# RWKV-7 recurrence on one Trainium2 core: state steps moved into the windows, forward group n beside backward group 0, 4, 3, 2, 1

## The reference

```python
def _rwkv7_step(state, inp):
    r, w, k, v, kk, a = inp
    sa = jnp.einsum("dbhvk,dbhk->dbhv", state, kk)
    state = (state * w[..., None, :] - sa[..., None] * (kk * a)[..., None, :]
             + v[..., None] * k[..., None, :])
    return state, jnp.einsum("dbhvk,dbhk->dbhv", state, r)
...
    _, y = lax.scan(_rwkv7_step, s0, (shared(r), to_scan(decay), to_scan(k_dir),
                                      shared(v), shared(kk), to_scan(iclr)))
    y = y[0] + _seg_flip(y[1], n_ctx, 1)
```

## Time and profile before

| | us |
|---|---|
| median of three executions | 6579.88 |
| the profiled execution, own time | 6581.77 |
| its span (first to last instruction) | 6579.9 |
| its mean granted TensorE clock | 0.935 of full |
| busy in the span: TensorE | 5670.6 (86%) |
| busy: VectorE / ScalarE / GpSimd | 2987.5 / 2063.0 / 1877.6 |

### The profile page before, as it was taken

One profiled execution on the slowest core, in us unless ns is written; L12 is line 12 of the kernel. 1 busy time (PEld: TensorE's weight loads), 2 busy tenths in 40 slices (PEclk: granted clock), 3 DMA queues, 4 the chain that ended last, 5 costly groups with the idle time before them and its releaser, 6 DMA issues. The chain is left out here.

```text
span 6579.9 us, 214205 instructions
## 1 busy us (share of the span) xinstructions
PE 5670.6 (86%) x92720; PEld 3807.5 (58%) x92720; DVE 2987.5 (45%) x6387; ACT 2063.0 (31%) x3451; POOL 1877.6 (29%) x2006
## 2 busy tenths in 40 slices
PE   5999788888887899977888895698999888888887
PEld 4555577777774455444554454544454677777773
DVE  7100366666663233145534367522300466666661
ACT  3000255454541312133422132311100354544440
POOL 4452144444441336000002631000000344444440
PEclk8999899999998999988899997899999899999998
DMA  3222100001112222122212237522112001110002
GB/s 130 100 90 84 45 31 31 31 31 43 36 37 76 106 100 79 44 84 68 60 48 91 95 96 96 127 72 85 65 65 74 35 31 39 37 39 31 31 31 93
DMA packets 192660, 425.81 MB, mean 65 GB/s; under 512 B 24384, under 2 KB 108224, under 8 KB 192192
## 3 DMA queue, kind: packets, MB, share of 16 engines
q1 hardware_dynamic: 157440, 322.85, 16.5%
q10 hardware_dynamic: 34752, 96.51, 3.7%
HBM read 313.41 MB, written 105.87 MB: 64 GB/s over the span
## 5 line engine op out<-in xcount | busy, mean ns | idle before, releaser
L382 PE MATMUL ps<-arena 128*128 128x512 f32 x4544 | 1686.0, 533 | 60.4 <-ACT arena L336 18.4
L382 PEld LDWEIGHTS ps<-arena 128*128 128x128 f32 x4544 | 862.9, 190 | 878.7 <-issue 810.5
L1890 PE MATMUL ps<-arena 64*64 64x64 f32 x35840 | 737.1, 226 | 172.1 <-issue 75.9
L158 POOL TENSOR_TENSOR arena<-arena 128x512 f32<-128x512 f32 (+1 forms) x360 | 338.9, 957 | 1700.3 <-DMA arena<-w_mod 1690.1
L1890 PEld LDWEIGHTS ps<-arena 64*64 64x64 f32 x35840 | 644.3, 138 | 244.7 <-issue 229.9
L2297 ACT COPY arena<-ps 128x512 f32<-128x512 f32 (+1 forms) x880 | 535.8, 626 | 411.7 <-PE ps L1890 403.1
L2442 POOL TENSOR_TENSOR arena<-arena 128x256 f32<-128x256 f32 (+1 forms) x320 | 316.6, 997 | 812.5 <-DVE arena L2683 533.7
L540 PE MATMUL ps<-arena 128*128 128x512 f32 (+1 forms) x1152 | 422.9, 527 | 18.2 <-ACT arena L336 18.2
L2367 POOL MEMSET arena<- 128x1280 f32 (+4 forms) x22 | 15.1, 739 | 1331.2 <-POOLq L88 1331.2
L161 POOL TENSOR_TENSOR arena<-arena 128x256 f32<-128x256 f32 (+2 forms) x504 | 376.5, 759 | 51.2 <-issue 0.2
L1698 ACT COPY arena<-ps 128x1280 f32<-128x1280 f32 (+1 forms) x64 | 75.0, 1172 | 963.5 <-PE ps L382 749.0
(11 more groups left out here) (269 smaller groups left out, 9762.3 us busy)
## 6 DMA issues: line engine op xcount, KB each, us to landing
arena<-proj SPq DMA_DIRECT2D x158, 640.0 KB, 5.1
proj<-arena ACTq DMA_DIRECT2D x80, 640.0 KB, 3.8
arena<-w_mod SPq DMA_DIRECT2D x96, 512.0 KB, 7.4
arena<-rw_w SPq DMA_DIRECT2D x68, 512.0 KB, 3.4
xres<-arena ACTq DMA_DIRECT2D x24, 640.0 KB, 6.1
arena<-na_w_in SPq DMA_DIRECT2D x24, 512.0 KB, 3.6
arena<-x SPq DMA_DIRECT2D x16, 640.0 KB, 6.7
arena<-xres SPq DMA_DIRECT2D x16, 640.0 KB, 6.0
```

The source lines that it names most:

```text
L158: self.nc.gpsimd.tensor_tensor(out, strip[:, c:c + n, :], self.k.cond[:, c:c + n, s:s + 1].to_broadcast([P, n, P]), ALU.mult)
L382: last = nc.tensor.matmul(k.ps[:, 3 * u + n, 0:b - a], w[:, c * P:(c + 1) * P], src[:, c, a:b], start=(c == 0), stop=(c == KT - 1))
L1890: last = PE.matmul(part_of(out, dst, hh, g, d), part(l, src, hh, g, d), rhs, start=True, stop=True)
```

## The change

It does the following in rwkv_recur; the diff is cut to its core.

- Window n of a tile now holds chunk group n in the forward direction and group BACK[n] = 0, 4, 3, 2, 1 in the backward one. So the order of the windows is the order of both recurrences.
- The state loop is gone. The four state steps of a window's chunks are issued in the next turn, between the products of that window; a last set of them stands behind the last tile. Each step has the same eight matmuls as before. The states restart at zero at each tile (restart()).
- Because the two directions of a window lie on different tokens, V is kept for both (four transposes of v in place of two) and local_outputs() goes per direction: 64 matmuls in place of 56 (16 chunks and directions). GpSimd no longer sums M3; it adds the second touch of y instead (second_outputs()).
- turned_scores() multiplies BH against KK and R in one set of sixteen 128-column matmuls; the set of 64 columns for the receptances (m4) is gone.
- Both halves of the negated gh, and the negated zt, are done by ScalarE; before, one half and zt were VectorE's.
- x4 also waits for nt_ev, f1 for y4_ev, kv for y_ev.
- Between two tiles there remain the projections, the key norm, the first operands and the normalisation of the tile before, in an order of their own. weighted() and finished() go to windows 0 and 1, the product of bonus_terms() to windows 2 and 3, gate_values() to window 0.
- The first tile's preparation is in the same loop body; LOOP_FILL is 70 in layer 0 and 69 in layer 3.

```diff
-LOOP_FILL = (0, 24)
+BACK = (0, 4, 3, 2, 1)
+LOOP_FILL = (70, 69)
...
+            def step(n):
+                for d in range(2):
+                    at, col = map_of(d, n) * C, chunk_of(d, n) * C
+                    for hp in HP:
+                        PE.matmul(state_reads(d)[hp, col:col + C], Sst[hp, n % 2, d, :], QT[hp, at:at + C], start=True, stop=True)
+                    for hp in HP:
+                        last = PE.matmul(state_sums(d)[hp, :], TT[hp, at:at + C], Sst[hp, n % 2, d, :], start=True, stop=True)
+                    last.then_inc(s_mm[d], 1)
...
             def turned_scores():
-                scores(low[1], BH_, KK_).then_inc(xt_mm, 1)
+                for d in range(2):
+                    for g in range(2):
+                        for hh in range(2):
+                            for c in range(2):
+                                at, col = (2 * g + c) * C, (g * 2 + d) * C
+                                last = PE.matmul(halves(pair[1][HP[c], hh, :])[:, :, col:col + C], ops[HP[hh], BH_, d, at:at + C],
+                                                 ops[HP[hh], KK_:R_ + 1, d, at:at + C], start=True, stop=True)
+                last.then_inc(xt_mm, 1)
...
                 pe.wait_ge(gh_ev, it + 1)
-                pe.wait_ge(gh1_ev, it + 1)
                 transitions()
                 pe.wait_ge(x2_ev, it + 1)
                 pe.wait_ge(x2t_ev, it + 1)
+                pe.wait_ge(nt_ev, it + 1)
                 product(low[0], B1, B0, 1).then_inc(x4_mm, 1)
-                pe.wait_ge(nt_ev, it + 1)
-                pe.wait_ge(m3_summed, it + 1)
                 local_outputs()
                 pe.wait_ge(y2_ready, it + 1)
                 pe.wait_ge(f0_ready, it + 1)
+                pe.wait_ge(y4_ev, it + 1)
-                product(low[3], Ya, F, 1).then_inc(f1_mm, 1)
+                product(low[0], Ya, F, 1).then_inc(f1_mm, 1)
...
                 product(low[0], Yb, F, 2).then_inc(f2_mm, 1)
-                scores(low[1], BH_, R_).then_inc(m4_mm, 1)
...
+                pe.wait_ge(yw_ev, it + 1)
+                pe.wait_ge(q_ev, it + 1)
+                step(0)
                 pe.wait_ge(f2_ev, it + 1)
                 product(low[0], F, None, 3).then_inc(di_mm, 1)
+                states_seen(it, 1)
+                step(1)
...
                 product(low[0], A0, NT, 4).then_inc(z_mm, 1)
                 product(low[1], NT, A0, 4).then_inc(zt_mm, 1)
+                states_seen(it, 2)
+                step(2)
...
                 product(low[1], B0, B1, 5).then_inc(z2t_mm, 1)
                 product(low[0], B1, B0, 5).then_inc(z2_mm, 1)
+                states_seen(it, 3)
+                step(3)
                 product(low[2], Ya, F, 5).then_inc(f3_mm, 1)
+                pe.wait_ge(y_ev, it + 2)
+                pe.wait_ge(v_kept, it + 1)
...
                 product(low[0], A0, A1, 6).then_inc(z4_mm, 1)
-                product(low[3], Yb, F, 6).then_inc(f4_mm, 1)
+                product(low[1], Yb, F, 6).then_inc(f4_mm, 1)
                 first_scores()
...
                 product(low[2], Ya, F, 7).then_inc(f5_mm, 1)
                 turned_scores()
...
+                    carried(late, it)
                     eyed(Yb, low[0]).then_inc(y4_ev, 1)
+                    queries(it)
+                    masked(M4, high[1], k.m_i).then_inc(m4_ev, 1)
                     masked(M1, low[2], k.m_s)
                     masked(M3, high[2], k.m_i).then_inc(m3_ev, 1)
+                    step(late, it, 0)
+                    step(late, it, 1)
+                    if n == 0:
+                        weighted(e)
+                    if n == 1:
+                        finished(e)
                     if n + 2 < NW2:
                         sums_scan(e, n + 2)
+                    step(late, it, 2)
                     if more:
                         operands_beta(e, n + 1)
-                    V.tensor_scalar(wide(B1), low[1], -1.0, None, ALU.mult).then_inc(zt_ev, 1)
+                    if n:
+                        step(late, it, 3)
+                    else:
+                        restart(it)
+                    state_outputs(late)
```

More of the change, by code:

```diff
@@ new lines, in queries, with step @@
+            def queries(it):
+                if it > 1:
+                    dve.wait_ge(r_kept, it - 1)
+                dve.wait_ge(yw_ev, it)
+                hold(k, dve)
+                V.tensor_tensor(QT.rearrange("p (c q) -> p c q", c=2), pair[3][:, :, 4 * C:8 * C],
+                                Rk.rearrange("p (c q) -> p c q", c=2), ALU.add).then_inc(q_ev, 1)
+            def step(unit, it, n):
+                for d in range(2):
+                    q = map_of(d, n)
+                    dve.wait_ge(s_mm[d], (it - 1) * 4 + (n + 1))
+                    V.scalar_tensor_tensor(Sst[:, (n + 1) % 2, d, :], state_sums(d), pc[:, unit, q:q + 1],
+                                           KHs[:, q * C:(q + 1) * C], ALU.mult, ALU.add).then_inc(s_ev[d], 1)
@@ L2627, in _, with restart, state_outputs @@
+            def restart(it):
+                for d in range(2):
+                    dve.wait_ge(s_mm[d], it * 4)
+                    V.memset(Sst[:, 0, d, :], 0.0).then_inc(s_ev[d], 1)
+            def state_outputs(unit):
+                for d in range(2):
+                    at = outputs_to(d, unit)
+                    V.tensor_tensor(at, at, state_reads(d), ALU.add)
+                dve.drain().then_inc(y_ev, 1)
+            kk_scaled(0)
             dve.wait_ge(zeroed, 1)
             for e in range(KT):
-                def eyed(out, in_):
-                    return V.tensor_tensor(out.rearrange("p (h q c) -> p h q c", h=2, c=C), in_.rearrange("p h (q c) -> p h q c", c=C),
-                                           k.eye2.unsqueeze(1).unsqueeze(1).to_broadcast([P, 2, 4, C]), ALU.add)
@@ new lines, in _ @@
+                sums_scan(e, 0)
+                sums_rest(e, 0)
+                for c in range(3):
+                    centred(e, MEAN_BANK, c)
+                for c in range(3):
+                    kk_unit(e, c)
+                bonus(e, BONUS_BANK, 0)
+                operands_beta(e, 0)
+                operands_kk(e, 0)
+                variance(e, VAR_BANK)
+                operands_r(e, 0)
+                bonus(e, BONUS_BANK, 1)
+                bonus(e, BONUS_BANK, 2)
+                post_inverse(e)
@@ L2739, in _ @@
+                for c in range(3):
+                    scaled(e, SCALE_BANK, c)
+                mask_scores(e, 0)
+                mask_turned(e, 0)
+                mask_rest()
+                operands_keys(e, 0)
+                sums_scan(e, 1)
+                sums_rest(e, 1)
                 for n in range(NW2):
                     window(n)
-                step(1)
-                kk_inverse(e + 1)
-                step(2)
-                carried(NW2 - 1)
-                step(3)
-                queries(NW2 - 1)
@@ L2793, in _ @@
-                mask_rest()
-                operands_keys(e + 1, 0)
-                sums(e + 1, 1)
+            it = KT * NW2 + 1
+            carried(NW2 - 1, it)
+            for c in range(3):
+                centred(KT, MEAN_BEFORE, c)
+            queries(it)
+            for n in range(4):
+                step(NW2 - 1, it, n)
+            state_outputs(NW2 - 1)
+            for c in range(3):
+                bonus(KT, BONUS_BEFORE, c)
+            variance(KT, VAR_BEFORE)
+            post_inverse(KT)
```

877 lines of the change are left out of this document (378 added, 499 removed).

## The result

The changed kernel took 7324.03 us (median of four executions, 7307.09 to 7337.58), the kernel before beside it 6577.11 us; the ratio is 1.1135 [1.111, 1.1159]. The forecast was 6532 us with a range of 6420 to 6650; the result lies far outside, and no rival reached it. The profiled execution took 7337.58 us, its span is 7335.4 us.

The account below looks back on a forecast made before the run. TensorE was taken to bound the windows. Per layer +3 (start), -147.7 (between tiles), +8.8 (window 0), +144 (windows 1 to 4), -32 (end): -23.9; twice, -48 from 6581.8 gives 6534, median 6532 us, range 6420 to 6650.

Parts of the forecast that it names:

- the window's sum: Windows 1 to 4: 19.7 us of TensorE work plus 4.4 of waits, 24.1, taken as 23.8 against 19.3 before.
- the slowest: Rival: state steps wait for each other and cost 1.3 us each, as alone; +224 us, 6756 us, chance 0.04.
- gh of window 4 to gh of the next window 0: Stretch across a tile boundary: 26.5 us between tiles and 30 for window 0, forecast 56.5 us.
- The walk of a window: New order followed from x2 through windows 1 to 4, wait by wait; new waits of 4.4 us in all.
- the sentence on GpSimd's 3 us instructions: Windows 0, 2 and 3 would lose something to GpSimd sharing SBUF interfaces with VectorE; no size given.
- The rival of VectorE's row: VectorE's late work behind step 3 leaves TensorE idle; 25.0 us a window, +96 us, 6628 us, chance 0.17.
- Full windows: Rival: windows about as full of TensorE work as before, 22.3 us each; -120 us, 6412 us, chance 0.26.
- Between the tiles: From gh's end to x2, a chain without the 19 steps: 26.5 us against 47.6 before, bounds 23 and 34.
- The low-clock rival: Half clock through the between-tiles chain into window 0; projections 7 us more a tile, +98 us, 6630 us, chance 0.09.
- Window 0: First window of a tile: 30 us against 28.9 before, including some 3.5 us of stalls on "issue".
- The start of a layer: First tile's preparation becomes the longer chain: +3 us a layer; filling matmuls taken as covered by loads and memsets.
- The end of a layer: From a layer's last window to the output projection: 60 us against 91.8 before, -32 us a layer.

Follow-up runs that it names:

- e3: Changed kernel with LOOP_FILL (77, 39) for (70, 69), placing both layers' window bodies within seven pieces of 256 instructions; 6676.93 us, ratio 1.0144.
- e6: e5 with TensorE's w group issued ahead of first_scores() in every window; 6605.48 us, ratio 1.0035.
- e9: e6 with gate_values() moved from window 0 to window 1 and LOOP_FILL (13, 39) for (77, 39); 6554.24 us, ratio 0.9955.
- e8: e7 with the four projections put ahead of the sums of norms on TensorE between tiles; 6641.89 us, ratio 1.0085.
- e5: e3 with GpSimd's gate_values(), bonus_half() and bonus_terms() moved to the gap ahead of keep_r(); 6665.2 us, ratio 1.0122.
- e7: e6 with gate_values() moved to window 1 and VectorE's scans for window 1 moved behind queries() in window 0; 6633.32 us, ratio 1.0075.

## Why the prediction was wrong

**The step that failed** is the window's sum, 23.8 us. The prediction read the stalls on "issue" in window 0, priced them at 3.5 us once a tile, and took none in windows 1 to 4, without a reason; before the change there are none there. It never asked why window 0 had them and the others not: window 0 is the first turn of a loop, whose program is being brought, and the others are its repetitions. The edit adds 106 instructions to that body, and what was a cost of the first turn became one of all five: windows 1 to 4 took 36.5 us in layer 0 and 33.6 in layer 3. The stalls cost 647 us of the 792 between forecast and result; the granted clock of 0.90 in place of 1.00 in these windows is part of that. No rival had this mechanism; the slowest, at 6756, was 568 us short. The rows were there to be read: the queue of kind "instruction", and a stall in the middle of a set.

Without the stalls the forecast would have failed too, by less: e3 took 6677 us, above the end of the range, and is slower than the kernel before where faster was forecast. **The other terms** show why, read in e3, against the forecast:

| term | forecast | e3 | on 16 tiles |
|---|---|---|---|
| window 1 to 4, mean | 23.8 | 24.55 | 64 x 0.75 = +48 |
| gh of window 4 to gh of the next window 0 | 56.5 | 61.2 | 14 x 4.7 = +66 |
| first gh of a layer, against before | +4 | +13.6 | 2 x 9.6 = +19 |
| last gh to the output projection | 60 | 61 | +2 |

That is 135 of the 145 us between the forecast and e3; the rest I haven't followed.

- **The walk of a window** was near in its sum and wrong in some of its places (waits read in tile 3, window 2 where no other is named). x4 started 3.5 us after x2 (3.4 forecast), f1 waited 0.28 (0.2), di 0.38 (0.45), z2t 0.33 (0.4). kv waited 0.2 in windows 2 and 3, 0.8 in window 1 and 0.6 in window 4 (1.0). first_scores() waited 1.2 to 1.4 in windows 1 to 3 and 0.6 in window 4 (0.9). The wait of f5, 1.24 to 1.44 us in two windows of four, was not in it: the sentence on GpSimd's 3 us instructions in windows 0, 2 and 3 named the places rightly, but stood as part of a rival and had no price of its own. The rival of VectorE's row had a real mechanism, and its windows of 24.4 us and more came true in e3 (24.55); but it wasn't what decided the result.
- **Full windows**, 22.3 us, came out nearly in e6 and e9 (22.9), after moves that the change did not make.
- **Between the tiles** the forecast missed 5.0 us of 31.5 in tile 3, and 4.0 us in the mean of the 14 stretches of e3 (30.5 us where 26.5 was forecast). In tile 3 TensorE stands 2.75 us on "issue" behind the loop's end, and the sums take 4.42 us in place of 2.2, at half clock; they end 7.2 us behind gh, where 2.2 were assumed. The low-clock rival was right that the clock falls, but it is down for part of the stage only. In four of the 14 stretches of e3 the clock stays up until the sums are almost done, and these are the shortest, 28.5 to 29.1 us; where it is at half through all of the sums, in six, the stage takes 31.5 to 32.0. So in this order the clock is worth 3 us a tile, not the 7 of the rival, and even the shortest stretches are 2 us over the forecast, with a stall of 2.8 to 3.0 us in each. e8 doesn't contradict this: it kept the clock up in nine stretches, but put the sums later at the same time. One of the four:

```profile
1728.30:1756.80 28.50, 23.29 (x161) 15.32 (x161) 13.35 (x27) 18.65 (x26) 8.72 (x7) 0.94 0.13 48
```

- **Window 0** was forecast at 30. The tiles shown took 30.2 in the changed kernel and 31.0 in e3; the means of 14 are 29.7 and 30.6.
- **The start of a layer** was priced at +3 us. The first tile now does the whole preparation, and LOOP_FILL is not covered (the prediction named this case, at some 8 us once, and left it out of the sum): the first sums begin at 768.94 with 77 filling matmuls and at 762.12 with 13, where they wait for ScalarE.

```profile
752.32 16.69 PE L2121 MATMUL ps<-arena 64*64 64x64 f32 x154 [11.86 <-POOLq L2363]
768.94 4.42 PE L390 MATMUL ps<-arena 128*128 128x2 f32 x20
```
```profile
762.12 4.43 PE L390 MATMUL ps<-arena 128*128 128x2 f32 x20 [7.61 <-ACT arena L2235]
```

- **The end of a layer**, 60 us, was met: 62 us in layer 0 of the changed kernel, 61 in e3, 91.8 before.

## What to carry to other kernels

Before a loop body grows, count its instructions, and look whether its repetitions run without stalls on "issue" where its first turn has some: such a difference can be the program being brought, as here, and it can come to every turn at once. The signs in a profile are a stall inside a set of like matmuls, equal numbers of instructions between stalls, and more packets in the instruction queue. An order written by hand is also judged by what else runs beside each instruction: moves of a few lines (e5 and e6) were worth 1.6 us a window. And look at all repetitions of a stage before one is taken for the rule: here a single tile hid that the clock fell in some and not in others.

## What the runs showed of the hardware that was not expected

- A body of 1791 instructions of TensorE ran at 24.6 us a turn when it lay within seven pieces of 256, and at 33.6 to 36.5 us when it ended 92 or 227 instructions past them; one of 1685 at 19.3 and 34.3 us. Two past cost nothing, and 46 past cost every second turn 12 to 14 us.
- In the windows 1 to 4 of the changed kernel a piece that was waited for cost 0.4 to 4.5 us, and one in window 4 up to 6.4. The return to the loop's first instruction cost 2.4 to 3.0 us in layer 0 and 3.2 to 3.8 in layer 3. In the changed kernel and in e3, 2.7 to 3.5 us stand where the loop ends and the code behind it begins.
- Behind a stall of 3 us the granted clock was 0.50 for 4.3 us and 0.59 for 6.2 with two-column matmuls next (e7, tile 3), and 1.00 over 8 us, the stall among them, with 512-column ones next (e8, tile 3). Neither is a rule: the clock was down through the sums in 12 of 14 stretches of e7 and down before they began in 5 of 14 of e8.
- A VectorE instruction with two SBUF inputs took 2.90 us beside one of GpSimd, and 0.43 alone.
